# A hybrid backbone on one core: the second mixer's weights laid out in 8 KB rows ahead of use

## What is computed

```python
# layer 1: windowed grouped-query attention, weights w_in (1024 x 1536), w_out (1024 x 1024)
q, k, v = split(a_lat @ w_in, (1024, 1280))
q, k = rope(q, cos, sin) * scale, rope(k, cos, sin)
k_c, v_c = split(a_ctx @ w_in[:, 1024:], (256,))
o = softmax(q k^T over window and context, with a sink per head) v
h_lat = h_lat + g1 * (o @ w_out)
...
# PEER, both layers, blocks of 128 tokens
act = gelu(einsum('td,thkd->thk', xb, u_tab[expert]))
y = einsum('thk,thkd->td', gate * act, v_tab[expert])
```

## Time and profile before

| | us |
|---|---|
| median of three executions | 4095.4 |
| lowest and highest | 4089.33, 4099.39 |
| the profiled execution | 4092.5 |
| its span, first to last instruction | 4090.8 |
| first dot product of the trunk | 547.1 |
| TensorE, VectorE, ScalarE, POOL busy | 2896, 2570, 1365, 1593 |

### The profile page before, as it was taken

The page is one execution under the profiler, slowest core; times in us unless marked ns, Lnnn a source line. Parts: engine busy times, 40 slices in busy tenths (PEclk is TensorE's granted clock), DMA queues, the critical chain, the costliest instruction groups (busy, mean ns, idle before and its releaser), DMA issues. The chain is left out here.

```text
span 4090.8 us, 41461 instructions
## 1 busy us (share of the span) xinstructions
PE 2896.1 (71%) x14677; PEld 981.6 (24%) x14677; DVE 2569.6 (63%) x5990; ACT 1365.2 (33%) x3356; POOL 1592.5 (39%) x1411
## 2 busy tenths in 40 slices
PE   4999856667668667666877687677868766766665
PEld 0794611111112111111232133122412311111110
DVE  3313378875874885785486566746765677587444
ACT  2220123333333323233253354333625423333222
POOL 0005024444444543443343344434435444444332
PEclk7998877778768668767878798788878877866666
DMA  9117279999999999999999999999899999999998
GB/s 363 52 62 279 101 291 421 421 414 421 416 408 393 420 413 385 421 420 390 348 369 335 395 388 349 368 375 376 330 334 400 371 373 421 421 420 410 421 421 340
DMA packets 231824, 1478.38 MB, mean 361 GB/s; under 512 B 30112, under 2 KB 30160, under 8 KB 60992
## 3 DMA queue, kind: packets, MB, share of 16 engines
q0 software_dynamic: 184704, 1342.31, 81.8%
q1 hardware_dynamic: 46800, 133.31, 9.5%
q10 hardware_dynamic: 112, 0.11, 0.0%
HBM read 1470.29 MB, written 5.34 MB: 361 GB/s over the span
## 5 line engine op out<-in xcount | busy, mean ns | idle before, releaser
L1422 PE MATMUL peer_py<-peer_ring,peer_diag 64*64 64x512 f32 x10240 | 1834.5, 815 | 981.2 <-ACT peer_diag L1231 908.0
L1179 POOL DMA_INDIRECT peer_ring<-in_uv_dram,peer_idx x1280 | 1461.5, 1142 | 2037.2 <-PE peer_py L1422 1893.1
L1691 DVE CUSTOM_DVE_ANT_0 peer_ring<-peer_ring,peer_f 128x1024 f32<-128x1024 f32 x1280 | 1554.1, 1226 | 824.0 <-DMA peer_ring<-in_uv_dram,peer_idx 809.0
L1227 ACT ACTIVATE peer_diag<-peer_stack,peer_u 128x64 f32<-128x64 f32 x1280 | 443.6, 347 | 2057.7 <-DVE peer_u L1691 2037.1
L1422 PEld LDWEIGHTS peer_py<-peer_ring,peer_diag 64*64 64x64 f32 x10240 | 350.7, 163 | 2311.8 <-ACT peer_diag L1231 1999.4
L1231 ACT ACTIVATE peer_diag<-peer_diag,peer_gate 128x64 f32<-128x64 f32 x1280 | 445.1, 348 | 46.6
L1392 PE MATMUL peer_pb<-arena,peer_fT 128*128 128x512 f32 x320 | 186.4, 674 | 1.2 <-ACT peer_fT L1199 1.2
L355 DVE TENSOR_TENSOR m_w_low<-m_w_low_plain,m_w_high 128x2048 fp32r<-128x2048 f32 x16 | 37.4, 2338 | 170.5 <-ACT m_w_high L350 170.5
L1553 PE MATMUL mix_ps<-mod_rows_sb,peer_mix_aT 128*128 128x512 f32 x128 | 87.5, 800 | 67.5 <-DMA mod_rows_sb<-in_od_w_out_dram 67.5
L1778 DVE CUSTOM_DVE_ANT_0 peer_mix_flat<-mix_ps,peer_mix_mask,peer_mix_sink 128x512 f32<-128x512 f32 (+1 forms) x64 | 52.2, 816 | 107.8 <-PE mix_ps L1506 97.6
L1691 DVE DVE_READ_ACCUMULATOR2_ANT peer_u<- 128x1 f32 x1280 | 105.1, 82 | 0.0
(11 more groups left out here) (208 smaller groups left out, 2745.0 us busy)
## 6 DMA issues: line engine op xcount, KB each, us to landing
mod_rows_sb<-in_ada_w_dram SPq DMA_DIRECT2D x33, 1024.0 KB, 5.0
peer_ring<-in_uv_dram,peer_idx POOLq DMA_INDIRECT x1280
mod_rows_sb<-in_od_w_in_dram SPq DMA_DIRECT2D x144, 128.0 KB
mod_rows_sb<-in_od_w_out_dram SPq DMA_DIRECT2D x128, 128.0 KB
arena<-in_ada_w_dram SPq DMA_DIRECT2D x15, 1024.0 KB, 16.2
m_w_low_plain<-in_ev_w_in_dram SPq DMA_DIRECT2D x12, 1024.0 KB, 5.2
arena<-in_peer_wq_dram SPq DMA_DIRECT2D x2, 4096.0 KB, 29.1
mod_rows_sb<-mod_rows SPq DMA_DIRECT2D x10, 512.0 KB, 6.7
```

Of the source, the lines that this page charges most:

```text
L1179: pool.indirect_dma_start(ring[:, n % RING], None, A["uv"], bass.IndirectOffsetOnAxis(idx[:, i % 2, hd, k:k + 1], 0)).then_inc(sem(f"lande ...
L1227: act.activation(diag[:, n % RING], stack[:], ACT.Gelu, scale=u[:, n % RING:n % RING + 1]).then_inc(sem("gelu"), 1)
L1422: ins = pe.matmul(PY[strip(c), r], diag[strip(r), n % RING], ring[strip(r), n % RING, D + c * HALF:D + (c + 1) * HALF], start=s == 0, stop ...
L1691: dve.tensor_tensor_reduce(x, x, f[:, i % 2], 1.0, 0.0, ALU.mult, ALU.add, u[:, n % RING:n % RING + 1]).then_inc(sem("dot"), 1)
```

## The change

`lay_pieces` is new: POOL issues fourteen DMAs from DRAM to DRAM, each waited for before the next, right behind `norm_shift` in the first mixer. They write two scratch tensors, `mix_in` (3 column blocks x 2 pieces) and `mix_out` (2 x 2 pieces), whose pieces are [128, 4, 512]: each partition's 8 KB, four steps, lie in one run. SP then loads a piece of 1 MB with one DMA. The ring has two pieces, one in the modulation rows and one in a tensor of its own, `mix_w`, for which `aT_own` and `tok` give up their space: both product inputs and the norm lie in `flat`, rope's products go straight to `tok`, its second term and the output's `tmp` lie in `hot`, and attention's output goes back into `qT`. TensorE waits for a piece and counts it once in four steps. VectorE takes the output product 5 slots behind its last step in place of 2, and the second norm of tile 4 is due at slot 106 of tile 5 in place of 100.

```diff
+def lay_pieces(queue, S, A, mix_in, mix_out):
+    laid = 0
+    def copied(to, src):
+        nonlocal laid
+        queue.dma_start(to, src).then_inc(S("mix_laid"), 16)
+        laid += 16
+        queue.wait_ge(S("mix_laid"), laid)
+    for c in range(3):
+        for g in range(PER):
+            copied(mix_in[c, g], A["od_w_in"][0].rearrange("(g k p) n -> g p k n", g=PER, p=P)[g, :, :, c * HALF:(c + 1) * HALF])
+    for c in range(2):
+        for g in range(PER):
+            q, j = divmod(g * WG, 4)
+            for x in range(2):
+                src = A["od_w_out"][0].rearrange("(q x j n) w -> q x n j w", q=2, x=2, j=4)
+                copied(mix_out[c, g, x * HD:(x + 1) * HD], src[q, x, :, j:j + WG, c * HALF:(c + 1) * HALF])
...
             norm_shift(pool, S, T, a, rows)
+            lay_pieces(pool, S, A, mix_in, mix_out)
...
+WG = 4
+PER = KC // WG
-W_RING = 4
+W_RING = 2
...
-        w = rows[:, 1, 1:3].rearrange("p a n -> p (a n)").rearrange("p (r n) -> p r n", r=W_RING)
+        w_own = sb("mix_w", [P, WG, HALF])
+        w = (rows[:, 1, 1:3].rearrange("p a (k n) -> p (a k) n", n=HALF), w_own[:])
...
-        aT_own = sb("mix_aT", [P, KC, P])
-        tok = sb("mix_tok", [P, 2, HALF])
...
-        aT = (aT_own, flat[:, 0:D].rearrange("p (k n) -> p k n", k=KC))
-        t1, t2, tmp = (flat[:, D + x * HALF:D + (x + 1) * HALF] for x in range(3))
+        aT = [flat[:, x * D:(x + 1) * D].rearrange("p (k n) -> p k n", k=KC) for x in range(2)]
+        norm = flat[:, 2 * D:3 * D]
+        tok = norm.rearrange("p (a n) -> p a n", a=2)
+        tmp = hot[:].rearrange("p a b c -> p (a b c)")
-        oT = aT_own
...
             def in_pieces(c):
-                for k in range(KC):
+                for g in range(PER):
                     to, loaded = next_slot()
-                    for x in range(2):
-                        at_row = k * P + x * HD
-                        sp.dma_start(to[x * HD:(x + 1) * HD], A["od_w_in"][0][at_row:at_row + HD, c * HALF:(c + 1) * HALF]
-                                     ).then_inc(loaded, 16)
+                    sp.dma_start(to, mix_in[c, g]).then_inc(loaded, 16)
...
+            sp.wait_ge(S("mix_laid"), 16 * (3 + 4) * PER)
             in_pieces(KV)
...
-                if first:
-                    pe.wait_ge(S(f"mix_w{n % W_RING}"), 32 * (n // W_RING + 1))
-                return w[:, n % W_RING]
+                if first and k % WG == 0:
+                    pe.wait_ge(S(f"mix_w{n % W_RING}"), 16 * (n // W_RING + 1))
+                return w[n % W_RING][:, k % WG]
...
-                    if x == len(parts) - 1:
+                    if x == len(parts) - 1 and k % WG == WG - 1:
                         pieces += 1
                         ins.then_inc(S("mix_w_used"), 1)
...
-                    ins = pe.matmul(PM[:, c], oT[:, m], weights, start=m == 0, stop=m == PAIRS - 1)
-                    pieces += 1
-                    ins.then_inc(S("mix_w_used"), 1)
+                    ins = pe.matmul(PM[:, c], qT[b % 2][:, m], weights, start=m == 0, stop=m == PAIRS - 1)
+                    if m % WG == WG - 1:
+                        pieces += 1
+                        ins.then_inc(S("mix_w_used"), 1)
...
-            def rope(ps, t, heads):
+            def rope(cosines, ps, t, heads):
...
+                tokens, t2 = cosines, tmp[:, 0:wide]
...
+                return dve.tensor_tensor(tokens, tokens, by_head(t2), ALU.add)
...
-                    yield out_slot(b, PAIRS * (c + 1) - 1) + 2
-                    dve.wait_ge(S("mix_w_used"), OUT_PIECES[b] + (c + 1) * PAIRS)
+                    yield out_slot(b, PAIRS * (c + 1) - 1) + 5
+                    dve.wait_ge(S("mix_w_used"), OUT_PIECES[b] + (c + 1) * PER)
```

More of the change, by code:

```diff
@@ L431, with mixer0_stage @@
 SC = P + SEQ
[L434 removed]
+def lay_pieces(queue, S, A, mix_in, mix_out):
[14 more added lines that the diff above has]
+                copied(mix_out[c, g, x * HD:(x + 1) * HD], src[q, x, :, j:j + WG, c * HALF:(c + 1) * HALF])
+def mixer0_stage(nc, S, A, h, ident, silu, mod_d, strips_d, arena, rows, mix_in, mix_out):
     n_in = 6
@@ L942 @@
             (KV, ((5, 1, 0),), at(6, 15)), (Q0, ((4, 0, 1), (5, 1, 3)), at(6, 21)), (Q1, ((4, 0, 0), (5, 1, 2)), at(6, 32)))
-PRODUCT_PIECES = (8, 16, 24, 32, 40, 64, 88, 96, 104)
-OUT_PIECES = (40, 64, 104, 120)
+WG = 4
+PER = KC // WG
+PRODUCT_PIECES = tuple(PER * n for n in (1, 2, 3, 4, 5, 8, 11, 12, 13))
+OUT_PIECES = tuple(PER * n for n in (5, 8, 13, 15))
 ATTENDS = (at(4, 50), at(5, 30), at(6, 50), at(7, 8))
@@ L980, in key_tiles, with trunk_stage @@
     return list(range(CT)) + [CT + j for j in range(lo, hi)]
-def trunk_stage(nc, S, A, h, ident, mod_d, arena, rows):
+def trunk_stage(nc, S, A, h, ident, mod_d, arena, rows, mix_in, mix_out):
     with ExitStack() as ctx:
@@ L1426, in _, with piece @@
             pieces = 0
-            def piece(first):
+            def piece(k, first):
                 n = pieces
-                if first:
-                    pe.wait_ge(S(f"mix_w{n % W_RING}"), 32 * (n // W_RING + 1))
-                return w[:, n % W_RING]
+                if first and k % WG == 0:
+                    pe.wait_ge(S(f"mix_w{n % W_RING}"), 16 * (n // W_RING + 1))
+                return w[n % W_RING][:, k % WG]
             def normed(j, tile, to, start):
@@ L1460, in product_of @@
                             pe.wait_ge(S("mix_kT"), tile + 2)
-                    weights = piece(x == 0)
+                    weights = piece(k, x == 0)
                     ins = pe.matmul(PM[:, bank], aT[to][:, k], weights, start=k == 0, stop=k == KC - 1)
-                    if x == len(parts) - 1:
+                    if x == len(parts) - 1 and k % WG == WG - 1:
                         pieces += 1
@@ L1551, in outputs @@
                         pe.wait_ge(S("mix_oT"), PAIRS * (b + 1))
-                    weights = piece(True)
-                    ins = pe.matmul(PM[:, c], oT[:, m], weights, start=m == 0, stop=m == PAIRS - 1)
-                    pieces += 1
-                    ins.then_inc(S("mix_w_used"), 1)
+                    weights = piece(m, True)
+                    ins = pe.matmul(PM[:, c], qT[b % 2][:, m], weights, start=m == 0, stop=m == PAIRS - 1)
+                    if m % WG == WG - 1:
+                        pieces += 1
+                        ins.then_inc(S("mix_w_used"), 1)
             def mixer():
@@ L1746, in keys_roped @@
                         dve.wait_ge(S("mix_tabs"), 64)
-                    rope(ps[:, 0:KV_HEADS * HD], tile - CT, KV_HEADS)
-                    dve.tensor_tensor(tok[:, x, 0:KV_HEADS * HD], t1[:, 0:KV_HEADS * HD], t2[:, 0:KV_HEADS * HD], ALU.add).then_inc(S("mix_k"), 1)
+                    straight = tok[:, x, 0:KV_HEADS * HD].rearrange("p (x j n) -> p x j n", x=2, n=HD)
+                    rope(straight, ps[:, 0:KV_HEADS * HD], tile - CT, KV_HEADS).then_inc(S("mix_k"), 1)
                 dve.wait_ge(S("mix_k"), tile + 1)
@@ L1762, in queries_roped @@
                     dve.wait_ge(S("mix_qT_ps"), n - 1)
-                rope(PM[:, bank], tile - CT, 8)
-                def paired(y):
-                    return y.rearrange("p (x j n) -> p x j n", x=2, j=4)
-                dve.tensor_tensor(tok[:, x].rearrange("p (j x n) -> p x j n", j=4, x=2), paired(t1), paired(t2), ALU.add).then_inc(S("mix_q"), 1)
+                paired = tok[:, x].rearrange("p (j x n) -> p x j n", x=2, n=HD)
+                rope(paired, PM[:, bank], tile - CT, 8).then_inc(S("mix_q"), 1)
                 dve.wait_ge(S("mix_q"), n + 1)
@@ L1924, in backbone @@
         modulation_stage(nc, S, A, h, ident, silu, mod_d, strips_d, arena, rows_flat)
-        mixer0_stage(nc, S, A, h, ident, silu, mod_d, strips_d, arena, rows)
-        trunk_stage(nc, S, A, h, ident, mod_d, arena, rows)
+        mix_in = nc.dram_tensor("mix_in", (3, PER, P, WG, HALF), F32).ap()
+        mix_out = nc.dram_tensor("mix_out", (2, PER, P, WG, HALF), F32).ap()
+        mixer0_stage(nc, S, A, h, ident, silu, mod_d, strips_d, arena, rows, mix_in, mix_out)
+        trunk_stage(nc, S, A, h, ident, mod_d, arena, rows, mix_in, mix_out)
         final_stage(nc, S, A, h, out)
```

21 lines of the change are left out of this document (8 added, 13 removed).

## The result

| | us |
|---|---|
| median after, of four executions | 3967.13 (3961.07 to 3974.07) |
| median before, of the executions beside them | 4092.36 (4089.28 to 4099.39) |
| ratio, with its 95% interval | 0.9692 (0.9669 to 0.9716) |
| the profiled execution after, and its span | 3970.96, 3969.2 |
| first dot product of the trunk (before 547.1) | 551.0 |

The kernel became 3.1% faster, by 125 us. The time lies 13 us under the forecast and inside its range, and the direction is right. The experiments will show that the reason I gave for most of it is not the right one.

What follows compares the result with a forecast made beforehand. The trunk was taken as bound by DMA, the mixer costing it bytes, bandwidth and idle time. 4092.5 us less 115 for streamed loads, other terms nothing, gave 3977.5, written as 3980 for the median; range 3940 to 4050.

Steps and rivals of the forecast that it cites:

- 100 us of slow packets: Mixer-weight stretches of the trunk: of 134 us above peer_wq's rate, 100 us were put down to slow packets.
- Streamed loads: Mixer weights in 34 DMAs of 1 MB with 8 KB rows, not 272 of 128 KB: saves 115 us, bounds 34 to 150.
- two neighbouring windows: SP-queue loads beside the gathers: 2 KB rows at 340 GB/s, then peer_wq in 4 KB rows at 416 GB/s.
- The sum of 115: Saving forecast in the trunk's weight stretches: 134 us at peer_wq's rate, less 19 us that stay for the engine mix.
- 34 us on idle engines: Five weight stretches with DMA share below 1.02: 34 us of the 134 were counted as idle engine time.
- Rival A: Weight stretches: row size brings nothing and only the idling goes, 34 us, so 4062 us; chance 0.07.
- Two pieces on chip: Output stages: third piece wanted 6.5 us after issue, lands in 7.5; 1 us waiting in each of four, covered by the ring.
- Rival B: Refills of the two buffers: 1 MB pieces come late, 5 us at each of 16, 80 us back, 4041 us; chance 0.08.
- VectorE's three slots, buffers: Taking the output product three slots later and the moved buffers cost nothing; VectorE's 114.5 us wait should mostly go.
- The copies: Fourteen DRAM to DRAM copies on POOL take 97 to 164 us, inside its 196.8 us gap, and cost nothing.
- Rival C: Copies overrun POOL's gap and delay mixer 0; at 312 us the gain is eaten, at 350 us 4133; chance 0.04.
- sign of a broken cover: After the copies: convolution starting after 314 us, or TensorE waiting for mixer 0's weights, would show the cover wrong.

## Why the prediction came out right, and where it was wrong

The time came out right in part by luck: the sum was near, but its largest term, 100 us of slow packets, rests on a cause that the runs refute.

*What bounds the kernel.* The trunk is bound by DMA, and the gain came from the stretches with streamed weights. The forecasts by tile were near: 375 for tiles 4 and 6 (378.6, 373.5), 350 for tile 5 (353.2), 338 for tile 7 (343.8), rate over 400 in the stretches with weights (418 and 420 in slots 24 to 60 of tile 4, but 392 in the last 42 us of its output stage), gather packets of 320 ns (315), TensorE's waits under 30 us (18.6), VectorE's under 40 (gone), 17,000 packets fewer (16,864).

*Streamed loads: the step that failed.* It is the sentence "A second stream does not slow the gathers; rows of 2 KB in small DMAs do", and the claim before it that two neighbouring windows tell size and queue apart. They differ in span too, and the span is the cause. Four runs say so: 8 KB rows with 64 partitions gain 5 us at most (4090.6), 2 KB rows with 128 partitions gain 88 us (4004.4 and 4006.9), and the old kernel with the span alone gains 83 (4012.1). Of the 125 us, by the runs on the buffers of after, 90 come with the span at 2 KB rows (4097.3 to 4006.9) and 40 with the longer rows (4006.9 to 3967.1), which is 5 more than the whole because the old loads on the new buffers lie 3 to 5 us above the kernel before; at 64 partitions the same longer rows are worth 7 (4097.3 to 4090.6). The sum of 115 held, since I took the rate of peer_wq's window as the target and not a price per packet, and the real change had both properties of that window. Had the change relaid the weights and kept two DMAs of 64 partitions, I would have forecast the same 3980 and missed by 110 us. The sign of being wrong that I gave for this step, stretches that stay near 340 GB/s, could not catch it, since the change altered the span together with the rows.

*Idle and slow packets.* I put 34 us on idle engines and 100 on slow packets. The waits for weights fell by 102.6 - 18.6 = 84 us, and the time by 125, but waits and slow packets overlap: the pieces come late because the rate is low. One run says that idling is no term of its own. With two DMAs of 64 partitions and 8 KB rows the waits for weights are 41.7 us in place of 102.6, and the idling in the first output stage is gone; yet the stage takes what it took. From slot 106 to the end of tile 4, before and with those loads:

```profile
2204.80:2282.30 77.50, 48.69 (x192) 12.00 (x188) 43.84 (x111) 17.10 (x45) 21.65 (x20) 0.77 0.91 322
...
2211.30:2288.90 77.60, 48.17 (x204) 12.53 (x200) 44.08 (x111) 17.32 (x45) 20.91 (x22) 0.71 1.02 340
```

The share rises from 0.91 to 1.02 and nothing is saved: the time that was idle is filled by slow packets. So in these runs the 34 us came only together with the wider span.

*Rival A* was right that row size is not what makes the packets slow, for a reason that it did not name, and wrong that 34 us would come of the idling nevertheless: with 64 partitions it goes, and the time is 4090.6, not 4062. The Trainium skill's least transfer for line rate (DMA: Bandwidth & Descriptors, Specifications, 512 B) which I had dismissed by the earlier trace rows is borne out better than I wrote: 2 KB rows run at 416 GB/s at full span. What they cost, 37 us, goes with later landing; more was not shown of it.

*Two pieces on chip.* The mechanism was right, and both of its terms were off. A refilled piece lands in 9.0 us, not 7.5, by the page's DMA issues after:

```profile
mod_rows_sb<-mix_in SPq DMA_DIRECT2D x9, 1024.0 KB, 9.0
...
peer_mix_w<-mix_in SPq DMA_DIRECT2D x9, 1024.0 KB, 9.4
...
mod_rows_sb<-mix_out SPq DMA_DIRECT2D x8, 1024.0 KB, 9.0
```

And it is wanted sooner than I had it. SP issues the third piece of the first output stage here:

```profile
2183.50 0.32 SPq L1109 DMA_DIRECT2D mod_rows_sb<-mix_out  x1
```

The second four steps take 3.60 us and the combine 1.09, so TensorE wants the piece at 2187.9, 4.4 us later and not 6.5; it has it at 2192.6, 9.1 us after the issue. So this stage waits 4.7 us, not 1, and the four together 18.6, not 4. Rival B's 80 us did not come: two-tile products show no wait at all.

*VectorE's three slots, buffers.* Nothing that can be measured, as said: taking it 2 behind gives 3964.2, and the new buffers with old loads give before's time (4097.3).

*The copies.* No cost that can be measured, as said (4094.67 with them alone, ratio 0.9997), and cheaper than my bounds of 97 to 164 us. The issues of the two tensors after (durations in ns, first and last start, then landing):

```profile
L441 POOL DMA_DIRECT2D mix_in<-in_od_w_in_dram x6: 703/704/899, 116.7 to 149.2; - x6
...
DMA to landing us min/median/max: 5.3/5.8/8.0
...
L441 POOL DMA_DIRECT2D mix_out<-in_od_w_out_dram x8: 577/577/578, 154.8 to 188.2; - x8
```

POOL's timeline after, the convolution behind them:

```profile
315.63 2.21 POOL L563 TENSOR_SCALAR m_aT_low_plain<-arena,m_cw 128x768 f32<-128x768 f32 x1 [126.86 <-DVE arena L780]
```

They ran from 116.7 to some 193, 76 us. I had taken the writing of a gather's rows by POOL, 0.95 us for 128, as the price of each 128 rows; a plain DMA is issued in 0.58 us with 256 rows and 0.70 with 512. POOL still waited 126.9 us for VectorE afterwards. The convolution began at 315.6 in place of 313.7, later than the 314 that I had named as a sign of a broken cover, and TensorE waited 1.1 us in place of 0.2 for the first mixer's weights:

```profile
PE m_ps L363 <- DVE m_w_low L355: 1.1, 1, 1.1
```

The sign was set too tight. Two other kernels with the same fourteen copies start the convolution at 313.8 and 314.1 (four DMAs of 128 partitions; 2 KB rows), so the two microseconds are not shown to be the copies' at all. Rival C with its 312 us was far away. The rule of the Trainium skill that I had weighed there (SBUF — State Buffer, the "DVE blocks DMA" trap) showed no price beyond those two microseconds. I expected 5000 more packets of 2 KB on q0; there were 2784 more, since 10.49 MB moved in 2560 packets of 4 KB.

## What to carry to other kernels

Look at how many partitions each load spans before looking at its rows: loads that covered 64 partitions or 16 slowed the full-width gathers beside them, and one DMA of 128 partitions in the place of two of 64 was worth 2% of this kernel without moving a buffer on chip. Look at the outermost dimension of the access pattern too: with a 2 there, two of the sixteen engines carried the load. Do not count idle time of a shared resource as a gain of its own: here it went and the time stayed, because slow packets filled it. And when a fast stream in the trace is taken as the model for a slow one, list all in which the two differ (rows, size, span, queue, issue) and make the cheap run that changes one of them.

## What the runs showed of the hardware that I had not expected

- Beside gathers over 128 partitions, loads of 64 partitions with 8 KB rows bring the whole traffic to about 240 GB/s while they pass (420 with full span), at a DMA share of 1.0, and a gather's packet to 547 ns. With 2 KB rows the fall is shallower and longer, at the same cost over twelve slots (44 us in place of 36). Over those slots gather packets of 8 KB take 315 ns beside loads of 128 partitions (317 with 2 KB rows), 363 and 374 beside 64, 424 beside 16.
- A load whose source pattern begins with a dimension of 2 moves at 51 GB/s, a share of 0.13.
- A copy from DRAM to DRAM of 512 rows of 2 KB lands in 5.8 us beside other loads and moves in packets of 4 KB.
- A 1 MB load with 8 KB rows lands in 9.0 us beside saturating gathers (the medians of the four kinds of piece are 9.0 to 10.6), against 5.0 us for the modulation's loads.
